# Pool entry: ScalarE's product copies and one product's terms in other places, the second running-sum row behind the second quad's sums, a later wait for stored rows

## The reference

```python
def pool_mixer(x, w_in, w_grp, scale, w_out):
    h = x @ w_in                                   # 1024 x 1024 @ 1024 x 4096
    u, z = h[..., :D_POOL], h[..., D_POOL:]
    ...
    csum = jnp.cumsum(u, axis=1)
    for g, w in enumerate(POOL_WINDOWS):           # windows 2, 4, 8, 16
        outs.append((c - lag) / cnt - u[:, :, g])  # a running mean over w rows, minus u
    m = ...
    m = jnp.einsum('bsgc,gcd->bsgd', m, w_grp).reshape(B, S, D_POOL) * scale
    return (m * jax.nn.silu(z)) @ w_out
```

## Time and profile before

| | us |
|---|---|
| median of 3 runs | 1797.96 |
| lowest, highest | 1797.88, 1798.27 |
| the profiled execution, its own time | 1797.84 |
| its span in the profile | 1796.0 |
| PE busy in it | 1777.2 (99%) |
| DVE busy | 1410.6 (79%) |
| ACT busy | 690.0 (38%) |
| POOL busy | 1102.2 (61%) |

### The profile page before, as it was taken

One profiled execution on the slowest core, in us unless ns is written; L12 is line 12 of the kernel. 1 busy time (PEld: TensorE's weight loads), 2 busy tenths in 40 slices (PEclk: granted clock), 3 DMA queues, 4 the chain that ended last, 5 costly groups with the idle time before them and its releaser, 6 DMA issues.

```text
span 1796.0 us, 22436 instructions
## 1 busy us (share of the span) xinstructions
PE 1777.2 (99%) x8398; PEld 1485.6 (83%) x8398; DVE 1410.6 (79%) x1665; ACT 690.0 (38%) x1211; POOL 1102.2 (61%) x772
## 2 busy tenths in 40 slices
PE   9999999999999999999999999999999999999998
PEld 8888888888888888888888888887788888888886
DVE  7889877766696658666599989679888875798896
ACT  6555577843431111111233334414433343333314
POOL 4066632360399979888778778633655465567554
PEclk9999999999999999999999999999999999999999
DMA  7342410032303323233375631133232231943232
GB/s 210 95 154 57 126 34 17 22 125 94 128 27 103 129 71 118 96 116 117 106 281 179 231 129 48 48 98 90 94 123 100 106 141 71 366 173 107 73 102 94
DMA packets 142718, 206.53 MB, mean 115 GB/s; under 512 B 48897, under 2 KB 104833, under 8 KB 138897
## 3 DMA queue, kind: packets, MB, share of 16 engines
q1 hardware_dynamic: 142434, 205.03, 34.0%
q10 hardware_dynamic: 176, 0.07, 0.0%
HBM read 151.51 MB, written 53.04 MB: 114 GB/s over the span
## 4 chain that ended last, share of the span: by engine, by line
PE 77%; DVE 1%; ACT 1%; issue 0%; POOL 0%; DVEq 0%; ACTq 0%
PE ps L1392 68%; PE ps L1744 2%; PE ps L1746 2%; PE ps L1745 2%; PE ps L1978 1%; PE ps L1977 1%; PE ps L1979 1%; PE ps L1865 0%; ACT xs_hi L2553 0%; PE ps L1645 0%; PE ps L1731 0%; PE ps L1620 0%; PE ps L1635 0%; DVE xs_lo L3489 0%; POOL ring_lo L1327 0%
## 5 line engine op out<-in xcount | busy, mean ns | idle before, releaser
L1392 PE MATMUL ps<-f_hi,ring_hi 128*128 128x512 f32 x368 | 143.5, 390 | 0.0
L1392 PE MATMUL ps<-f_lo,ring_hi 128*128 128x512 f32 x368 | 143.3, 389 | 0.0
L1392 PE MATMUL ps<-f_hi,ring_lo 128*128 128x512 f32 x368 | 143.3, 389 | 0.0
L1238 POOL TENSOR_TENSOR ring_lo<-w_sum,ring_hi 128x512 fp32r<-128x512 f32 x84 | 128.4, 1529 | 7.0
L1392 PE MATMUL ps<-d_w_hi,d_hid_hi 128*128 128x512 f32 x312 | 121.6, 390 | 0.0
L2427 ACT ACTIVATE f_copy<-ps 128x512 f32<-128x512 f32 x63 | 37.3, 596 | 219.4 <-PE ps L1392 211.6
L1392 PE MATMUL ps<-d_w_hi,d_hid_lo 128*128 128x512 f32 x312 | 121.5, 389 | 0.0
L1392 PE MATMUL ps<-d_w_lo,d_hid_hi 128*128 128x512 f32 x312 | 121.5, 389 | 0.0
L1392 PE MATMUL ps<-f_low,ring_hi 128*128 128x512 f32 x336 | 117.2, 389 | 0.0
L1327 POOL TENSOR_TENSOR ring_lo<-w_sum,ring_hi 128x512 fp32r<-128x512 f32 x56 | 87.6, 1574 | 40.7 <-ACT ring_hi L2548 40.6
L1237 POOL TENSOR_SCALAR ring_hi<-w_sum 128x512 fp32r<-128x512 f32 x84 | 79.1, 942 | 31.3 <-PE ps L1392 30.2
(11 more groups left out here) (574 smaller groups left out, 5859.8 us busy)
## 6 DMA issues: line engine op xcount, KB each, us to landing
d_raw<-hid_rows SPq DMA_DIRECT2D x37, 512.0 KB, 4.4
stage<-in_w_up SPq DMA_DIRECT2D x22, 512.0 KB, 4.6
wd_raw<-in_w_down SPq DMA_DIRECT2D x22, 512.0 KB, 5.0
raw_w<-in_w_gate SPq DMA_DIRECT2D x20, 512.0 KB, 4.9
stage<-in_pool_w_in SPq DMA_DIRECT2D x16, 512.0 KB, 4.9
raw_w<-in_pool_w_in SPq DMA_DIRECT2D x16, 512.0 KB, 4.7
m_rows<-u_row SPq DMA_DIRECT2D x16, 512.0 KB, 2.6
z_rows<-z_buf SPq DMA_DIRECT2D x8, 1024.0 KB, 4.1
```

Source lines behind the costliest of these rows:

```text
L1238: g.tensor_tensor(view(lo), src, view(hi).bitcast(F32), ALU.subtract).then_inc(w_split, 1)
L1392: last = mm(out_ap, l, r, start=(start and j == 0), stop=(stop and j == n - 1), skip_group_check=onto)
```

## The change

Five edits, all at the entry of the pool mixer except the last:

1. PE: the product 2 of quad 0 is split. Its eight matmuls with the high part (`sum_high(2, 2)`) come ahead of product 4, its four with the low part (`sum_low(2)`) behind it.
2. ACT: the fourth part of sum 0 (`x_sum_hi(0)`) comes ahead of copy 0 of quad 0, and copy 1 of quad 0 comes behind the first part of sum 1, with the other three parts behind the copy.
3. ACT, quad 1: copy 0 waits for the first sum of quad 0 on DVE (L3256) where it waited for the second (L3262); the high part of one weight block follows it, then copies 1 and 2 behind the wait for the second sum, then the high parts of blocks 1, 2 and 3.
4. DVE, first pair: `window_rows(0, 1)` moves from ahead of quad 1's sums to between quad 1's `block_sums` and its two additions at L3275.
5. DVE, all later pairs: the wait for the stored rows (`m_stored`) moves from ahead of L3256 to behind it.

```diff
--- before.py
+++ after.py
@@ -1904,24 +1904,32 @@
 
             sum_of = {2: 0, 1: 1, 3: 2, 6: 3}
 
-            def sum_product(o, at):
+            def sum_high(o, at):
 
                 i = sum_of[o]
                 pe.wait_ge(w_split, IN_BLOCKS + blocks_split(N_QUADS) + at + 1)
                 if o >= 4:
                     pe.wait_ge(prod_copied, IN_COPIES + 3 * N_QUADS + o - 3)
                 pe.wait_ge(xs_hi_ready, 4 * i + 4)
-                (w_h, w_l), (x_h, x_l) = ring[o], x_sum[i]
+                (w_h, w_l), x_h = ring[o], x_sum[i][0]
                 dst = ps[:, bank_of[o], :]
                 for k in range(4):
                     cs = slice(k * P, (k + 1) * P)
                     mm(dst, w_h[:, cs], x_h[:, k, :], start=(o < 4 and k == 0), stop=False, skip_group_check=(o >= 4))
                     mm(dst, w_l[:, cs], x_h[:, k, :], start=False, stop=False, skip_group_check=(o >= 4))
+
+            def sum_low(o):
+
+                i = sum_of[o]
                 pe.wait_ge(xs_split, i + 1)
                 for k in range(4):
-                    last = mm(dst, w_h[:, k * P:(k + 1) * P], x_l[:, k, :], start=False, stop=(k == 3),
-                              skip_group_check=(o >= 4))
+                    last = mm(ps[:, bank_of[o], :], ring[o][0][:, k * P:(k + 1) * P], x_sum[i][1][:, k, :], start=False,
+                              stop=(k == 3), skip_group_check=(o >= 4))
                 last.then_inc(prod_full, 1)
+
+            def sum_product(o, at):
+                sum_high(o, at)
+                sum_low(o)
 
             def x_sums(o):
                 if o == 0:
@@ -1932,8 +1940,10 @@
                 if o == 5:
                     pe.wait_ge(x3_split, 12)
 
-            quad(N_QUADS, 0, x_factors, (0, 4), x_sums)
-            sum_product(2, 2)
+            quad(N_QUADS, 0, x_factors, (0,), x_sums)
+            sum_high(2, 2)
+            quad(N_QUADS, 0, x_factors, (4,), x_sums, at=1)
+            sum_low(2)
             quad(N_QUADS, 0, x_factors, (5,), x_sums, at=3)
             sum_product(1, 4)
             pe.wait_ge(sig_ready, 16)
@@ -2572,13 +2582,13 @@
                 act.wait_ge(prod_full, IN_BLOCKS + quad_full(q, o))
                 f(x_copy[:, j, :], ps[:, bank0 + o, :], ACT.Copy).then_inc(prod_copied, 1)
 
-            x_sum_hi(0, (0, 1, 2))
+            x_sum_hi(0)
             act.wait_ge(w_split, IN_BLOCKS + blocks_split(N_QUADS) + 7)
             copy_product(N_QUADS, 0, 0)
-            x_sum_hi(0, (3,))
             x3_part(15)
-            x_sum_hi(1)
+            x_sum_hi(1, (0,))
             copy_product(N_QUADS, 0, 1)
+            x_sum_hi(1, (1, 2, 3))
             pool_block_hi(1, 0)
             pool_block_hi(1, 1)
             x_sum_hi(2)
@@ -2624,13 +2634,20 @@
                     next_hi(q, 3)
                     first_block_rows(i)
                     next_hi(q, 4, 5, 6)
-                act.wait_ge(quad_summed, IN_SUMS + 4 * q + 2)
+                act.wait_ge(quad_summed, IN_SUMS + 4 * q + (2 if i else 1))
                 copy_product(q + 1, 4, 0)
-                next_hi(q + 1, 0, 1)
-                copy_product(q + 1, 4, 1)
-                next_hi(q + 1, 2)
-                copy_product(q + 1, 4, 2)
-                next_hi(q + 1, 3)
+                if i == 0:
+                    next_hi(q + 1, 0)
+                    act.wait_ge(quad_summed, IN_SUMS + 4 * q + 2)
+                    copy_product(q + 1, 4, 1)
+                    copy_product(q + 1, 4, 2)
+                    next_hi(q + 1, 1, 2, 3)
+                else:
+                    next_hi(q + 1, 0, 1)
+                    copy_product(q + 1, 4, 1)
+                    next_hi(q + 1, 2)
+                    copy_product(q + 1, 4, 2)
+                    next_hi(q + 1, 3)
                 if i == 7:
                     pool_rows_hi(0)
                 if i:
@@ -3555,18 +3572,21 @@
             rows = [u_row[b % 2][:, HALO + HALF * (b // 2):HALO + HALF * (b // 2 + 1)] for b in range(4)]
             for i in range(8):
                 q = N_QUADS + 2 * i
-                if i:
+                def rows_stored():
                     for c in range(2):
                         dve.wait_ge(m_stored[c], 16 * i)
-                quad_sums(q, 0, x_copy, rows, None if i == 7 else lambda: pool_sums(2 * i + 2))
+
+                quad_sums(q, 0, x_copy, rows, None if i == 7 else lambda: pool_sums(2 * i + 2),
+                          first=rows_stored if i else None)
                 dve.wait_ge(c11_ready, IN_QUADS + i + 1)
                 dve.wait_ge(quad_summed, IN_SUMS + 4 * q + 4)
                 window_rows(i, 0)
-                window_rows(i, 1)
                 if i:
+                    window_rows(i, 1)
                     dve.wait_ge(z_stored, 16 * i)
                 quad_sums(q + 1, 4, x_copy, [z_buf[:, b, :] for b in range(4)],
-                          first_rows_lo if i == 7 else lambda: pool_sums(2 * i + 3))
+                          first_rows_lo if i == 7 else lambda: pool_sums(2 * i + 3),
+                          low=None if i else lambda: window_rows(0, 1))
 
 
             def row_mean(t):
```

## The result

| | us |
|---|---|
| before, median of 12 runs | 1797.82 (1797.73 to 1798.27) |
| changed, median of 12 runs | 1801.65 (1800.90 to 1802.51) |
| ratio, 95% interval | 1.0021 (1.0013 to 1.0029) |
| changed, the profiled execution and its span | 1802.51 and 1800.7 |

The change makes the kernel 3.8 us slower. That is 2.2 us beyond the likeliest case (1799.5) and 0.05 us above the upper end of the forecast's whole range (1801.6). The profiled execution is the slowest of the twelve, so its rows show somewhat more than the median. The runs of the changed kernel spread over 1.6 us, those of before over 0.5.

A forecast was written before the change was run, and what follows sets the result against it. The prediction took DVE's chain, then ACT, to bound the kernel from 1253 to 1291.41. A chain 0.47 us later plus 1.05 for POOL made 1.5 us: 1797.84 + 1.5 = 1799.36, median 1799.5, range 1796.9 to 1801.6.

The forecast's parts named there:

- the likeliest case: Full clock throughout, DVE's chain later: 1799.5 us, own range 1798.6 to 1800.1, chance 50%.
- the stretch: From 1253 to 1291.41, ending at quad 2's product 5: DVE busy 34.35 of 35 us to 1288, then ACT.
- The distance of 4.58 us that the forecast hangs on: From the start of quad 1's additions at L3275 to PE's start of quad 2's product 5, claimed unchanged.
- the second rival: DVE's chain does not grow, POOL's instructions fall into gaps: -0.6 to +0.4 us, 1797.4 to 1798.4, chance 10%.
- both waits: PE's waits in quad 1 before products 4 and 5, 1.36 and 1.09 us, claimed to go.
- The POOL instruction met the four `xs_raw`: On DVE, POOL's low part of quad 1's block 1 falls among the four `xs_raw`, costing 1.1 us.
- The meeting: POOL's low part of block 4 beside DVE's moved running-sum instruction before L3275, claimed to cost 1.05 us.
- The sum at full clock: Product 5 of quad 2, and with it the kernel, 1.5 us later: 0.47 of DVE's chain plus 1.05.
- the rival's price: Clock falls in the wait at quad 2's product 5: 0 to 1.85 us, 1.7 taken, giving 1801.2; chance 35%.
- the 3.7 us: Time from PE's last matmul to the clock's fall at the span's end, taken as the wait length that decides.
- slower by over 0.2%: Whole kernel slower than 1801.6 us, needing the clock's full price on top, chance 10%.
- The third rival: Each copy is there when PE comes: up to 5.4 us gained, 1792.6 us, chance 5%.

The follow-up runs named there:

- 20 matmuls in the wait: Changed kernel plus 20 matmuls of no use where PE stood idle ahead of quad 2's product 5: 1799.50 us.
- the last repair: Changed kernel with ACT's quad 2 copies 1, 2 before two Silus, earlier quad 4 load and even-quad copy 0, sum 1's parts before quad 0's copy 1: 1794.17 us.
- the first repair: Changed kernel with ACT's copies 1 and 2 of quad 2 and three weight blocks' high parts ahead of the Silus of blocks 2 and 1: 1799.16 us.
- the repair without edit 4: Changed kernel without edit 4, with ACT's copies 1, 2 of quad 2 ahead of two Silus, earlier quad 4 weight load and even-quad copy 0: 1799.65 us.
- one place with 3.04 us idle in its profile: Changed kernel plus 8 matmuls of no use where PE stood idle ahead of quad 2's product 5: 1800.89 us.

## Why the prediction was right, and where it was not

- **What bounds the stretch.** Right. DVE's chain up to quad 1's additions, then ACT up to copy 1, set product 5 of quad 2. The distance of 4.58 us that the forecast hangs on measured 4.57 (1288.44 to 1293.01), and 4.58 with edit 4 alone.
- **Edits 1 and 2.** Right. Forecast starts 1236.54, 1243.04 and `xs_lo` of sum 2 at 1253.36; measured 1236.56, 1243.06 and 1253.39. The POOL instruction met the four `xs_raw`: 3.58 us. Alone the edits cost 0.5. With that the second rival, a chain of DVE that does not grow, is out.
- **Edit 3.** Right that both waits go and are found again later. Alone it costs 0.9 between medians, and nothing in the two executions whose clock stayed up.
- **Edit 4.** Right. Forecast: additions at 1288.35; measured 1288.44. The meeting cost 1.10 (2.33 for 1.23), where I took 1.05. The Trainium skill's rule (SBUF — State Buffer, "Who interferes with whom") names the right partners. The prediction took its price as the whole POOL instruction, but POOL's had begun 0.21 us ahead of DVE's (1283.26 and 1283.47): up to its end at 1284.70 1.23 us were left. Paid were 1.10, about as near to that as to the 1.05 from the rows.
- **Edit 5.** Right, nothing.
- **The sum at full clock.** 1.5 forecast, 1.56 measured with 20 matmuls in the wait.
- **The likeliest case.** Wrong. I gave 50% to a full clock and 35% to its fall, and it fell. My own range for that case ended at 1800.1. What failed is the rival's price and its chance. Its chance was too low by my own working: the wait of 4.9 us was past the 3.7 us from which I had it decide, and the prediction names nothing that would keep the clock up. The 3.7 us were too long as well: I read the time to the fall in one place as the idle time that it needs, and idle times of 2.3 and 2.7 us were enough elsewhere. For the price, I bounded the lower level by those 3.7 us, half of it lost, 1.85 at most. It lasted from 1291.6 to 1298.5, 5.5 us of it with PE at work, and cost 2.5 us in the profiled execution and 2.2 between medians. That error of size made "slower by over 0.2%" 10%, and it is what happened, at 0.21%. This rival's own sum ended at 1801.35 (1799.5 and 1.85). That the whole range missed by only 0.05 us is luck: it reached to 1801.6 for no reason in the rival.
- **The third rival**, all waits closed, could not come with this order on ACT. I said that only a shorter chain of DVE would speak for it. No chain became shorter in the last repair: with another order on ACT and SyncE 3.8 of the 5.4 us came.

## What to carry to other kernels

When an engine that is 99% busy shows short waits, ask for each which chain ends it, and whether the same chain has a later end: a wait ahead of the last one only spends time early. Closing the early ones gathers them into one long wait, and here a long wait of TensorE cost more than its short pieces: 2.2 us of clock on top in the changed kernel, 0.9 with edit 3 alone. A copy that an engine makes for PE should not stand behind instructions that wait for another engine's later results.

## What the runs showed that I had not expected

- The clock can fall after PE is at work again. In the first repair PE was idle from 1323.5 to 1325.78, 2.3 us, and the clock was at 0.52 in the slice that begins at 1327. Slices of that kernel (length, PE busy, instructions, granted clock, DMA share, GB/s):

```profile
1326.00:1327.00 1.00, 1.00 (x5) 1.00 0.95 393
1327.00:1328.00 1.00, 1.00 (x4) 0.52 1.26 393
1328.00:1329.00 1.00, 1.00 (x4) 0.50 0.60 120
1329.00:1330.00 1.00, 1.00 (x4) 0.50 1.05 347
1330.00:1331.00 1.00, 1.00 (x5) 0.77 1.08 382
```

- Idle times of 1.69 and 1.75 us left it full in the profiled executions; 2.32, 2.71, 3.04, 3.18 and 4.84 did not. The lower level then lasted some 3.4 us in all but the last, where it lasted 6.8. It began between 2.6 us (edit 3 alone) and 4.4 us (the repair without edit 4) after PE's last matmul had ended. What decides is open; one place with 3.04 us idle in its profile gave times from 1799.43 to 1802.48, and with 2.71 two of eleven executions kept the full clock.
- At the lower level matmuls of 512 columns followed each other by 0.43 us, at the full by 0.23: less than twice.
- The same edit (4) cost 1.1 us with one order on ACT and brought 4.8 with another.
